# Stick-breaking heads of a two-block kernel in pairs: scores, exponentials, logarithms and running sums of two heads side by side

## What is computed

```python
z = einsum('bhqd,bhkd->bhqk', q_blk, k) * scale
log_beta = log_sigmoid(z)
log_keep = where(mask, log_sigmoid(-z), 0.0)
log_survive = reverse cumsum of log_keep, shifted by one key
a = where(mask, exp(log_beta + log_survive), 0.0)      # then a @ v
...
f = lb + (1.0 - lb) * sigmoid(f_hg)
cum = cumsum(log(f))  within chunks of 64; decays are exp of differences of cum
```

## Time and profile before

| | |
|---|---|
| Median of 3 runs | 1595.55 us (1595.25 to 1600.18) |
| Profiled execution | 1595.38 us, its span 1593.6 us |
| TensorE busy | 1402.7 us (88%) |
| VectorE, ScalarE, GpSimd busy | 871.5, 578.8, 478.4 us |
| Mean granted TensorE clock | 0.979 of full speed |

### The profile page before, as it was taken

One profiled execution on the slowest core, in us unless ns is written; L12 is line 12 of the kernel. 1 busy time (PEld: TensorE's weight loads), 2 busy tenths in 40 slices (PEclk: granted clock), 3 DMA queues, 4 the chain that ended last, 5 costly groups with the idle time before them and its releaser, 6 DMA issues.

```text
span 1593.6 us, 17624 instructions
## 1 busy us (share of the span) xinstructions
PE 1402.7 (88%) x6500; PEld 845.1 (53%) x6500; DVE 871.5 (55%) x2048; ACT 578.8 (36%) x1078; POOL 478.4 (30%) x379
## 2 busy tenths in 40 slices
PE   6999999998878777878777777779999999899997
PEld 3888766697743232322222222226778987455544
DVE  2699675554659999844444444444437532412113
ACT  2244364433433433433333333335485411212112
POOL 0556400165533333333333333330435500000000
PEclk9999999999999999999999999999999999999999
DMA  9457521052379999999999999997133247799994
GB/s 384 189 233 292 211 93 67 25 214 103 135 299 422 421 421 421 421 421 422 421 421 422 422 421 421 421 411 298 53 141 124 107 167 310 280 427 428 428 427 199
DMA packets 53076, 475.86 MB, mean 299 GB/s; under 512 B 6144, under 2 KB 6784, under 8 KB 7552
## 3 DMA queue, kind: packets, MB, share of 16 engines
q0 software_dynamic: 36864, 268.45, 40.6%
q1 hardware_dynamic: 14832, 203.46, 31.8%
q10 hardware_dynamic: 1296, 2.84, 0.5%
HBM read 473.68 MB, written 1.05 MB: 298 GB/s over the span
## 4 chain that ended last, share of the span: by engine, by line
PE 52%; DMA 32%; DVE 10%; ACT 4%; issue 2%; POOL 1%; SPq 0%; DVEq 0%; ACTq 0%; POOLq 0%
DMA arena<-in_uv,pick 26%; PE psD L607 15%; PE psD L680 8%; PE psD L1103 6%; PE psY L853 5%; PE psD L685 4%; DVE arena L1911 4%; PE psD L1112 3%; ACT arena L1226 2%; DMA arena<-in_experts 2%; DMA ring<-in_w_mod 2%; PE psY L788 2%; DMA ring<-in_w_in 2%; PE psD L803 1%; PE psY L773 1%
## 5 line engine op out<-in xcount | busy, mean ns | idle before, releaser
L853 PE MATMUL psY<-arena 128*128 128x512 f32 x1024 | 513.4, 632 | 135.8 <-ACT arena L1226 133.9
L853 PEld LDWEIGHTS psY<-arena 128*128 128x128 f32 x1024 | 183.1, 196 | 462.6 <-ACT arena L1226 310.1
L1635 POOL DMA_INDIRECT arena<-in_uv,pick x256 | 240.7, 940 | 397.6 <-PE psY L853 372.8
L1226 ACT ACTIVATE arena<-cst,pick 128x128 f32<-128x128 f32 x256 | 102.9, 402 | 396.8 <-DVE pick L1911 393.8
L1911 DVE CUSTOM_DVE_ANT_0 arena<-arena,psD 128x1024 f32<-128x1024 f32 x128 | 156.3, 1221 | 162.5 <-DMA arena<-in_uv,pick 162.5
L1911 DVE CUSTOM_DVE_ANT_0 arena<-arena,psY 128x1024 f32<-128x1024 f32 x128 | 154.7, 1216 | 86.2 <-DMA arena<-in_uv,pick 85.6
L1226 ACT ACTIVATE arena<-psD 64x512 f32<-64x512 f32 (+4 forms) x128 | 68.3, 538 | 286.4 <-PE psD L1103 105.5
L1226 ACT ACTIVATE arena<-arena 128x128 f32<-128x128 f32 (+3 forms) x299 | 129.7, 434 | 17.1 <-DVE arena L2260 3.8
L1656 POOL TENSOR_TENSOR ring_r<-ring,work_r 128x1024 fp32r<-128x1024 f32 x19 | 46.5, 2460 | 159.1 <-ACT work_r L1226 159.0
L607 PE MATMUL psD<-arena 128*128 128x256 f32 (+4 forms) x352 | 90.3, 399 | 4.0 <-ACT arena L1226 2.4
L1752 DVE SCALAR_TENSOR_TENSOR psY<-arena,pick,psY 128x256 f32<-128x256 f32 x224 | 89.2, 482 | 0.0
(11 more groups left out here) (381 smaller groups left out, 2390.2 us busy)
## 6 DMA issues: line engine op xcount, KB each, us to landing
arena<-in_experts SPq DMA_DIRECT2D x30, 2048.0 KB, 19.9
ring<-in_w_in SPq DMA_DIRECT2D x18, 2048.0 KB, 10.0
ring<-in_experts SPq DMA_DIRECT2D x18, 2048.0 KB, 18.2
ring<-in_w_mod SPq DMA_DIRECT2D x12, 2048.0 KB, 9.3
ring<-in_w_pq SPq DMA_DIRECT2D x4, 2048.0 KB, 7.9
ring<-in_w_out SPq DMA_DIRECT2D x3, 2048.0 KB, 8.1
ring<-in_w_pw SPq DMA_DIRECT2D x2, 2048.0 KB, 8.1
ring<-in_w_o SPq DMA_DIRECT2D x2, 2048.0 KB, 10.6
```

The source lines that it names most:

```text
L853: last = nc.tensor.matmul(y_of[t][:, h * 512:(h + 1) * 512], diag[:, q % DIAGS, :], seats[q % SEATS][:, D + h * 512:D + (h + 1) * 512], st ...
L1226: return nc.scalar.activation(dst, src, f, **kw)
L1635: nc.gpsimd.indirect_dma_start(seats[q % SEATS], None, w["uv"], bass.IndirectOffsetOnAxis(index[:, q:q + 1], 0)).then_inc(gathered[q % SEA ...
```

## The change

The list is written pair by pair. Before, it is z0 z1, then p0 l0 z2, p1 l1 z3, p2 l2 z4, p3 l3 z5, p4 l4 z6 sig, p5 l5 z7 f ln, p6 l6 silu scan decay, p7 l7. Now it is z0 z1, then p0 l0 l1 p1 z2 z3, p2 l2 l3 p3 z4 z5, p4 l4 l5 p5 z6 z7 sig f ln, p6 l6 l7 silu scan decay p7. ScalarE makes |z| of both heads of a pair, then both exponentials, then both logarithms, with two new semaphores in place of `seq`.

```diff
-    for h in range(SBH):
-        order += [("p", h), ("l", h)]
+    for h in range(0, SBH, 2):
+        order += [("p", h), ("l", h), ("l", h + 1)]
+        if h == 6:
+            order += [("silu", 0), ("scan", 0), ("decay", 1)]
+        order.append(("p", h + 1))
         if h + 2 < SBH:
-            order.append(("z", h + 2))
-        order += {4: [("sig", 0)], 5: [("f", 0), ("ln", 0)], 6: [("silu", 0), ("scan", 0), ("decay", 1)]}.get(h, [])
+            order += [("z", h + 2), ("z", h + 3)]
+        if h == 4:
+            order += [("sig", 0), ("f", 0), ("ln", 0)]
...
-                    z = sbz[:, n % 2]
-                    seq(fn(z[:, 0, :], ps[:, 0:3 * P], ACT.Abs))
-                    seq(fn(z[:, 1, :], z[:, 0, :], ACT.Exp, scale=-1.0))
-                    fn(z[:, 1, :], z[:, 1, :], ACT.Ln, bias=1.0).then_inc(sp_ready, 1)
+                    fn(sbz[:, n % 2, 0, :], ps[:, 0:3 * P], ACT.Abs).then_inc(z_size, 1)
+                    if n % 2:
+                        for j in range(2):
+                            act.wait_ge(z_size, n + j)
+                            fn(sbz[:, j, 1, :], sbz[:, j, 0, :], ACT.Exp, scale=-1.0).then_inc(z_exp, 1)
+                        for j in range(2):
+                            act.wait_ge(z_exp, n + j)
+                            fn(sbz[:, j, 1, :], sbz[:, j, 1, :], ACT.Ln, bias=1.0).then_inc(sp_ready, 1)
```

More of the change, by code:

```diff
@@ L480, in build @@
         dl_ready, el_ready, xl_ready = sem("dl_ready"), sem("el_ready"), sem("xl_ready")
+        z_size, z_exp = sem("z_size"), sem("z_exp")
         sp_ready, nk_ready, arg_ready, a_exp, a_masked = (
```

## The result

The changed kernel takes **1605.12 us** (median of 5 runs, 1604.57 to 1606.96) where the kernel before takes 1595.95 us (5 runs on the same chip, 1595.25 to 1600.18): a ratio of **1.0065**, with a 95% interval of 1.0047 to 1.0083. It is 9.2 us slower. The forecast was 1601.2 us with a range up to 1604.5, so the direction was right and the time lies 0.6 us outside the range.

What follows compares the result with a forecast made beforehand. TensorE was taken as the bound. Terms -0.5, -1.7, +1.1, +2.6 and +0.4 put tile 5's end at +1.9 us; the scan's +8.8 less 3.0 slack gave 5.8, so 1595.4 + 5.8 = 1601.2 us, range 1597.2 to 1604.5.

Steps and rivals of the forecast that it cites:

- Start: Heads 0 and 1: head 0's sum begins at 1145.5 instead of 1144.72, tile 1 at 1147.8 instead of 1148.28: -0.5 us.
- Table loads: ScalarE: seven loads of 1.28 us go, 9.0 us, or 18.6 us with a drain; nothing gained on the path.
- Scores side by side: TensorE, tile 1 to tile 5: four lone scores (3.4 us) become two overlapping pairs (1.7 us), -1.7 us.
- Heads 2 and 3: TensorE waits 1.1 us for head 2's sum and 2.6 us for head 3's, whose masked share GpSimd holds.
- Rival 1: GpSimd also gets ahead of head 1's masked share, costing 2.5 us: 8.3 us in all, 1603.7 us; chance 0.24.
- rival 2: Head 3's step begins before GpSimd, 0.4 us instead of 2.6: sum 3.7 us, 1599.1 us; chance 0.14, mixed case 0.06.
- Heads 4 and 5: GpSimd idle by then: second sum waits 0.4 us, and tile 5 ends at +1.9 us.
- Heads 6 and 7, and the scan: Scan queued behind head 6's mask, held by GpSimd, begins 8.8 us later; less 3.0 us slack, 5.8 us.
- Sum: Whole kernel: profiled execution of 1595.4 us plus 5.8 us gives 1601.2 us; chance 0.36.
- Every sign that the prediction named: Scan at 1205 to 1210, mask 2 us or more, share about 2.5, level 0 wait near 5, 49 loads.
- Rival 3: GpSimd holds neither head 3's step nor the scan's prerequisites: level 0 at +1.8 us, 1597.2 us; chance 0.10.
- Rival 4: TensorE's idle time and the scores' overlap all won, 5.0 us faster, 1590.4 us; chance 0.03.

Runs made afterwards that it cites:

- the sums apart: Changed kernel with each odd head's sum moved back behind its odd projection tile, scores and ScalarE steps still paired: 1591.35 us, ratio 0.9983; measured again, 0.9984.
- The run with two small copies: Changed kernel plus two one-column copies on ScalarE between tile 2's copy and its roundings, so GpSimd starts later: 1599.21 us, ratio 1.0021.
- unread products: Changed kernel plus products nobody reads in three TensorE waits (ahead of head 3's sum, tile 6 and level 0's second half): 1600.66 us, ratio 1.0034.
- The last run: Kernel with odd sums behind their odd tiles, and sigmoid, f, its logarithm and the scan moved behind head 4's sum: 1590.97 us, ratio 0.9965.
- the scan ahead: Changed kernel with silu, scan and decay moved ahead of head 7's sum: 1599.39 us, ratio 1.0026.
- the triangle in PSUM: Changed kernel with the masked share's triangle copied once into PSUM, leaving that step one SBUF operand: 1600.94 us, ratio 1.0030; with the scan also moved, 1594.47 us.
- the serial ScalarE: Changed kernel's order, but ScalarE makes abs, exponential and logarithm one head after the other as before the change: 1609.23 us, ratio 1.0093.

## Why the prediction was right, and where it was wrong

| step of the prediction | forecast | measured |
|---|---|---|
| Start: tile 1 begins | -0.5 us | -0.47 (9.88 for 10.35 behind the first scores) |
| A pair of scores | 0.86 us | 0.86 |
| Wait ahead of head 2's sum | 1.1 us | 0.78 |
| GpSimd and head 3's share, from tile 1's end | 8.5 and 8.7 us | 8.53 and 8.57 |
| Wait ahead of head 3's sum | 2.6 us | 2.41 |
| Wait ahead of head 5's sum | 0.4 us | 0.17 |
| Tile 5 ends | +1.9 us | +4.35 (53.47 for 49.12) |
| Scan begins | +8.8 us | +10.9 |
| First decay exponential | +5.8 us | +7.9 |
| Wait in level 0 | near 5 us | 4.85 |
| Level 1 begins | +5.8 us | +10.5 |

All shifts in the table are counted from the first scores.

- **Table loads.** 49 instead of 56, as said. "Worth nothing" is wrong: with the order held fixed the joint steps are worth 4.6 us of stage in the changed order, and 2.9 with the sums apart, since they shorten the chains that TensorE waits for at its tightest places. The sum did not suffer by it, because the waits in it were worked out with the joint steps in place. A load costs its 1.28 us and no drain shows beside it: in the changed kernel an exponential ends at 1197.07, the load runs from 1197.09 to 1198.37, and the next function starts at 1198.38.
- **Scores side by side, Start, Heads 2 and 3.** Right in place and size, the held share of head 3 included. Its order was forecast with 0.2 us to spare and came with 0.04; that of head 1 was forecast with 0.01 and came with 0.03. That both orders came as forecast is in part luck: head 3's step began 0.13 us earlier than forecast, three times the margin that was left. Rival 1 was that near. The run with two small copies shows that head 3's order decides 4.7 us of stage; rival 2 put it at 2.15, the hold without the clock.
- **Heads 4 and 5.** Tile 5's end is off by 2.4 us. The clock behind head 3's wait took 2.7.
- **Heads 6 and 7, and the scan.** Right in its mechanism: the mask of head 6 waits for the exponential, is held, and the scan stands behind it. The shift of 2.1 us beyond the forecast is the one of tile 5, carried along. The half clock in tile 6 costs nothing more, as told at the end.
- **Sum. This is the step that failed.** It adds waits at their own length, and lets TensorE do everything between and behind them at the speed of the earlier trace rows. The missing term is what TensorE's clock takes after a wait: 2.7 us in head 3's sum and tile 3, 2.5 in level 0 and tile 8, 5.2 in all, less 0.5 from steps forecast a little too long, which makes 10.5 out of 5.8. The runs show it from both sides: unread products give back 2.7 and 2.5 us with all causes of waits in place, and removing a hold of 2.2 us gives 4.8 and 4.9 us in A. No wait of the earlier trace rows for TensorE was over 1.7 us and the clock in the earlier trace rows was 1.00, so no row of this stage had a price for it; but the mean granted clock of 0.979 said that elsewhere in the kernel it was not full, and I did not look there. Every sign that the prediction named came true (the scan at 1209.22 behind a mask of 2.31 us, the share of 2.58 us, waits of 2.41 and 4.85 us, 0.86 us for each pair, 49 loads): they ask for the waits, and none asks for the clock behind them.
- **Rival 3** (neither held) was put at +1.8 us, 1597.2. Not run in that form; with the share unheld but the mask of head 6 still held, the median is 1600.94.
- **Rival 4** (faster) asked for "sums that never wait and an early scan". The rows gave no room for either in the changed order, and that was right; in other orders there was some. The last run is such a one, at 1590.97 us. That this is near the 1590.4 of the rival is chance: it is another order, and its waits of 0.71, 0.31, 1.13, 1.36 and 0.41 us are still there.

## To carry to other kernels

When an edit puts a wait of some 2 us or more ahead of TensorE's work (here 1.83 us was the shortest with half clock behind it), price the work behind it at both clocks, and read the granted clock of the stretch in question and of others before calling a wait its own length. Pairing work pays where its consumers stay apart: give each sum a tile between it and its input, and let nothing that waits for a late exponential stand ahead of a step that others need. Where two starts on VectorE and GpSimd lie within a few tenths of a microsecond, treat both orders as open, since each may move a chain by several microseconds (4.7 us of stage here).

## What the runs showed of the hardware

**A wait's length alone does not decide on the clock.** Level 0 in two kernels, waits of 2.20 and 2.19 us; first the one with the scan ahead:

```profile
1210.63 1.16 PE L991 MATMUL psD<-arena 64*128 64x128 f32 x16 [2.20 <-ACT arena L1232]
```

Then the one with the triangle in PSUM as well:

```profile
1207.79 2.08 PE L991 MATMUL psD<-arena 64*128 64x128 f32 x16 [2.19 <-ACT arena L1232]
```

The same sixteen products take 1.16 us in the one and 2.08 in the other. In the changed order with the serial ScalarE, waits of 2.87 us (1149.75) and 2.19 us (1187.01) have full clock behind them too, and one of 2.91 (1167.63) has not: tile 3 behind it starts its products 0.21 us apart. Ahead of tile 6 the wait is 1.83 us in several kernels; with the triangle in PSUM (1191.04) the clock is full behind it, in the changed kernel (1193.49) it falls after four products. What tells them apart the rows do not show, and I leave it open; for a forecast it means a cost that comes or doesn't, 1.5 to 2.7 us each time where it came.

**A subtraction of GpSimd that starts 0.04 us ahead is enough** for one instruction of VectorE to take 2.58 us instead of 0.42, and one operand moved to PSUM is enough to undo it.

**Half clock in a stretch that waits anyway costs nothing.** From the start of tile 6 to the sum of head 6 the changed kernel takes 7.32 us, and the one with the triangle in PSUM 5.83 at full clock. From the end of tile 5 to the first half of level 0 it is 19.06 us in both, because TensorE waits there for ScalarE (1.32 us in the one, 1.88 in the other).
